# Two transformer blocks on one core: the values of the second block's layers computed with tokens in rows, in 512-column products

## The reference

```python
h = rms_norm_2(x, pre_norm[l]) @ w_in[l]          # 256 x 3072, split in ten parts
dq, dk, dv, dgate, gq, gk, gv, ggate, mq, mgate = ...
# D: 6 heads of differential attention (two softmaxes a head, q and k of 32), rope on dq and dk
oa = rms_norm_2(diff_attention(q1, q2, k1, k2, dv, lam), diff_subln[l]) * silu(dgate)
# G: 6 query heads of 64 on 2 key/value heads, rms norm and axial rope on gq and gk
ob = gqa_attention(gq, gk, gv) * silu(ggate)
# M: 4 heads that read a memory of 256 rows
om = softmax(mq @ mk.T / 8) @ mv * silu(mgate)
x = x + rms_norm_2(concat(oa, ob, om) @ w_out[l], post_norm[l])
```

## Time and profile before

| | before |
|---|---|
| median of three runs | 712.62 us (711.74 to 713.48) |
| span of the profiled execution | 709.0 us |
| PE busy | 640.6 us (90%) |
| DVE busy | 354.9 us (50%) |
| ACT busy | 331.0 us (47%) |
| POOL busy | 45.9 us (6%) |

### The profile page before, as it was taken

How to read it: one execution, slowest core, us unless ns; L and a number is a source line. 1 busy time by engine, 2 the same in 40 slices (tenths; PEclk the granted TensorE clock), 3 DMA queues, 4 the chain that set the end, 5 groups by cost and what they waited for, 6 DMA issues and landing times.

```text
span 709.0 us, 11877 instructions
## 1 busy us (share of the span) xinstructions
PE 640.6 (90%) x4645; PEld 491.1 (69%) x4646; DVE 354.9 (50%) x820; ACT 331.0 (47%) x782; POOL 45.9 (6%) x57
## 2 busy tenths in 40 slices
PE   5989999999999999778686899999989999999996
PEld 4967898779743345323242589878878898888886
DVE  1543657555740131011010448889775577897743
ACT  3465655641120132111120344779865546888842
POOL 6001000000000000000000233010000020100000
PEclk9999999999999999897899999999999999999999
DMA  9994335597999999999999938018533071093101
GB/s 288 328 320 150 119 119 178 172 330 275 367 361 414 389 419 409 415 410 415 410 413 413 323 121 279 18 42 256 179 119 119 2 238 60 1 297 119 61 1 59
DMA packets 82169, 166.80 MB, mean 235 GB/s; under 512 B 4286, under 2 KB 59360, under 8 KB 78016
## 3 DMA queue, kind: packets, MB, share of 16 engines
q1 hardware_dynamic: 79984, 160.88, 62.8%
q0 software_dynamic: 2000, 5.06, 2.2%
q10 hardware_dynamic: 128, 0.08, 0.0%
HBM read 164.92 MB, written 1.07 MB: 234 GB/s over the span
## 4 chain that ended last, share of the span: by engine, by line
PE 59%; SPq 16%; DVE 9%; DMA 6%; ACT 6%; issue 3%; DVEq 0%; ACTq 0%
SPq L805 13%; PE psum L941 11%; PE psum L943 10%; PE psum L942 10%; PE psum L996 4%; DMA ring<-in_w_in_dram 3%; DMA ring<-in_w_expert_down_dram 3%; PE psum L1367 3%; PE psum L1258 3%; SPq L808 3%; PE psum L1305 2%; PE psum L1323 2%; DVE w_low L2414 2%; PE psum L1382 2%; PE psum L1350 2%
## 5 line engine op out<-in xcount | busy, mean ns | idle before, releaser
L941 PE MATMUL psum<-a_high,w_high 128*128 128x256 f32 x512 | 149.5, 292 | 5.4 <-ACT tiles L1617 1.7
L942 PE MATMUL psum<-x_low,w_high 128*128 128x256 f32 x512 | 144.7, 283 | 0.0
L943 PE MATMUL psum<-a_high,w_low 128*128 128x256 f32 x512 | 144.6, 283 | 0.0
L2414 DVE TENSOR_TENSOR w_low<-ring,w_high 128x1024 fp32r<-128x1024 f32 (+1 forms) x73 | 100.9, 1395 | 28.3 <-ACT w_high L1728 28.3
L941 PEld LDWEIGHTS psum<-a_high,w_high 128*128 128x128 f32 x512 | 97.8, 191 | 15.7 <-issue 7.2
L1728 ACT ACTIVATE w_high<-ring 128x1024 fp32r<-128x1024 f32 (+1 forms) x79 | 96.2, 1222 | 13.9 <-DMA ring<-in_w_in_dram 10.5
L942 PEld LDWEIGHTS psum<-x_low,w_high 128*128 128x128 f32 x512 | 98.0, 191 | 0.1
L943 PEld LDWEIGHTS psum<-a_high,w_low 128*128 128x128 f32 x512 | 98.0, 191 | 0.0
L1367 PE MATMUL psum<-ring,q_c 128*32 128x512 f32 x304 | 63.8, 700 | 22.3 <-DMA ring<-in_w_expert_up_dram 10.6
L941 PE MATMUL psum<-w_high,a_high 128*128 128x256 f32 x240 | 69.9, 291 | 1.8 <-DVE mix_low L2425 1.4
L2336 DVE TENSOR_TENSOR tiles<-tiles,psum 128x256 f32<-128x256 f32 x8 | 3.4, 421 | 127.5 <-ACT tiles L1784 127.5
(11 more groups left out here) (347 smaller groups left out, 1204.9 us busy)
## 6 DMA issues: line engine op xcount, KB each, us to landing
ring<-in_w_in_dram SPq DMA_DIRECT2D x36, 1024.0 KB, 8.0
ring<-in_w_expert_down_dram SPq DMA_DIRECT2D x24, 1024.0 KB, 17.0
ring<-in_w_expert_gate_dram SPq DMA_DIRECT2D x38, 512.0 KB, 14.7
ring<-in_w_expert_up_dram SPq DMA_DIRECT2D x38, 512.0 KB, 15.0
ring<-in_w_out_dram SPq DMA_DIRECT2D x12, 1024.0 KB, 5.4
ring<-in_w_mem_kv_dram SPq DMA_DIRECT2D x4, 1024.0 KB, 14.7
probs_values<-in_w_expert_down_dram SPq DMA_DIRECT2D x3, 1024.0 KB, 18.9
k_c<-in_w_expert_gate_dram SPq DMA_DIRECT2D x5, 512.0 KB, 8.9
```

The costliest lines, as they stand in the source:

```text
L941: pe.matmul(dst, left[0], right[0], start=first, stop=False)
L942: pe.matmul(dst, left[0], right[1], start=False, stop=False)
L943: return pe.matmul(dst, left[1], right[0], start=False, stop=last)
L2414: dve.tensor_tensor(w_l, raw_of(n), as_f32(w_h), ALU.subtract).then_inc(lows, 1)
```

## The change

The values are no longer four turned tiles with transposes. Two jobs `("nv", l, tt)`, one for each half of the tokens, compute all 512 value columns for 128 tokens: the tokens' high and low parts are the stationary operand, and the moving operand is one chunk of all four tiles' weights, 512 columns in four blocks of 128, which lie in four neighbouring places. It is again `product`, so 24 matmuls a job. ACT evicts the whole bank in one instruction. The weights of a value tile are split as before, now as `("v2", l, n)`, and all four splits must be there for the first job. The `nv` jobs stand in the turns of D0 and D1, tile 15 moves to D2, and its `hsq` and rope move back by a turn. `exchange` moves from D4 to D5. Column block 8 of the weights (with tile 16) is loaded before block 7.

```diff
-LOAD_ORDER2 = [0, 1, 2, 3, 4, 7, 8, 6, 9, 10, 5, 11]
+LOAD_ORDER2 = [0, 1, 2, 3, 4, 8, 7, 6, 9, 10, 5, 11]
...
-        tiles = [[6, 7], [8, 15], [16, 12], [13], [14], [17, 9], [18], [20], [19], [10], [22], [21], [11], [23], [], []]
+        tiles = [[], [], [15, 12], [13], [14], [17, 9], [18], [20], [19], [10], [22], [21], [11], [23], [], []]
+        values = [[("nv", l, 0)], [("nv", l, 1)]] + [[]] * (len(tiles) - 2)
...
-                if t in V_TILES:
-                    behind[n + 1].append(("vn", l, t))
...
-            turns.append((before[n] + [("tile2", l, t) for t in tiles[n]] + behind[n], s))
+            turns.append((before[n] + values[n] + [("tile2", l, t) for t in tiles[n]] + behind[n], s))
...
-LONG = ("tile1", "bv", "tile2", "mv")
+LONG = ("tile1", "bv", "tile2", "nv", "mv")
...
-        _at = max(_at, users(_n - 3)[0])
+        _at = max(_at, users(_n - (5 if SPLITS[_n][0] == "v2" else 3))[0])
...
+        def values_split(l, k):
+
+            a = units_before(SPLIT[("v2", l, V_TILES[0])]) % UNITS
+            assert a + len(V_TILES) <= UNITS
+            return [w[:, KC * P * a:KC * P * (a + len(V_TILES))].rearrange("p (n k q) -> p n k q", n=len(V_TILES), k=KC)
+                    [:, :, k, :] for w in (w_high, w_low)]
...
+            def values_product(dst, l, tt):
+
+                pe.wait_ge(lows, SPLIT[("v2", l, V_TILES[-1])] + 1)
+                own = slice(P * tt, P * tt + P)
+                for k in range(KC):
+                    mm = product(dst, (a_high3[:, k, own], x_low3[:, k, own]), values_split(l, k), k == 0, k == KC - 1)
                 return mm
...
-                elif kind == "vn":
-                    l, n = job[1:]
-                    from_act(("tile2", l, n))
-                    for tt in range(2):
-                        mm = pe.transpose(dst[:, P * tt:P * tt + P], tile3[:, n, P * tt:P * tt + P], ident)
+                elif kind == "nv":
+                    mm = values_product(dst, job[1], job[2])
...
-                elif kind == "vn":
-                    l, n = job[1:]
-                    op = act.activation(v2[:, :, V_TILES.index(n), :], src[:, 0:256].rearrange("p (t n) -> p t n", t=2),
-                                        ACT.Copy)
+                elif kind == "nv":
+                    op = act.activation(v_nat[:, 512 * job[2]:512 * job[2] + 512], src, ACT.Copy)
...
-                dve.wait_ge(p_act, taken(JOB[("vn", l, 16)]))
...
-                    if what[0] == "D" and what[2] == 4:
+                    if what[0] == "D" and what[2] == 5:
                         exchange(what[1])
```

More of the change, by code:

```diff
@@ L351, in item_of @@
         return [f"mem_{kind[1]}{job[1]}"]
-    if kind == "tile2":
+    if kind in ("tile2", "v2"):
         return [f"in{job[1]}_{job[2] // 2}"]
@@ L368 @@
 A_Q_TILES = (("tile1", 0), ("tile1", 1))
-OF_TILES, OF_ITEMS = ("tile1", "tile2"), ("bv", "y1", "y2")
+OF_TILES, OF_ITEMS, ONE_UNIT = ("tile1", "tile2"), ("bv", "y1", "y2"), ("tile1", "tile2", "v2")
 SPLITS = []
 for _job in JOBS:
-    _what = _job if _job[0] in OF_TILES else _job[:-1] if _job[0] in OF_ITEMS else None
-    if _what and _what not in SPLITS:
-        SPLITS.append(_what)
+    if _job[0] == "nv":
+        _parts = [("v2", _job[1], t) for t in V_TILES]
+    else:
+        _parts = [_job] if _job[0] in OF_TILES else [_job[:-1]] if _job[0] in OF_ITEMS else []
+    SPLITS += [what for what in _parts if what not in SPLITS]
 SPLIT = {what: n for n, what in enumerate(SPLITS)}
-UNIT_OWNER = [n for n, what in enumerate(SPLITS) for _ in range(1 if what[0] in OF_TILES else 2)]
+UNIT_OWNER = [n for n, what in enumerate(SPLITS) for _ in range(1 if what[0] in ONE_UNIT else 2)]
 def units_before(split):
@@ L385, in users @@
     what = SPLITS[split]
+    if what[0] == "v2":
+        return [JOB[("nv", what[1], tt)] for tt in range(2)]
     return [JOB[what]] if what[0] in OF_TILES else [JOB[what + (tt,)] for tt in range(2)]
@@ L395, in item_split @@
 def item_split(split):
-    return ITEM[item_of(SPLITS[split] if SPLITS[split][0] in OF_TILES else SPLITS[split] + (0,))[0]]
+    return ITEM[item_of(SPLITS[split] if SPLITS[split][0] in ONE_UNIT else SPLITS[split] + (0,))[0]]
 LAST_INPUT = max(n for n, _job in enumerate(JOBS) if _job[0] in ("tile1", "bv"))
@@ L508, in split_of @@
         def split_of(n):
-            wide = P if SPLITS[n][0] in OF_TILES else COLS
+            wide = P if SPLITS[n][0] in ONE_UNIT else COLS
             a = units_before(n) % UNITS * KC * P
@@ L522, in raw_of @@
                 return s.rearrange("p k (g m d) -> p k m g d", g=2, m=2)[:, :, what[1]]
-            return s[:, :, P * (what[-1] % 2):P * (what[-1] % 2) + P] if what[0] in OF_TILES else s
+            return s[:, :, P * (what[-1] % 2):P * (what[-1] % 2) + P] if what[0] in ONE_UNIT else s
         def split_like_raw(n):
@@ L966, in natural_product @@
                 return mm
+            def values_product(dst, l, tt):
[3 more added lines that the diff above has]
+                    mm = product(dst, (a_high3[:, k, own], x_low3[:, k, own]), values_split(l, k), k == 0, k == KC - 1)
+                return mm
             def output_product(dst, job, phase):
@@ L1274, in run_out @@
                 elif kind == "D":
-                    from_act(("vn", l, 6 + h // 2))
+                    from_act(("nv", l, 1))
                 elif kind == "G":
-                    from_act(("vn", l, 16))
+                    from_act(("nv", l, 1))
                 else:
```

## The result

| | before | after |
|---|---|---|
| median of five runs, us | 711.87 (711.13 to 713.48) | 715.93 (714.01 to 716.33) |
| span of the profiled execution, us | 709.0 | 714.3 |
| first product of tile 0, layer 0 and layer 1, us | 420.50, 566.59 | 422.32, 570.50 |
| from there to the first product of tile 20, us | 67.50, 66.81 | 69.66, 68.27 |

The ratio is 1.0058, with a 95% interval of 1.0039 to 1.0077: slower, by 4.1 us. The forecast was 710.8, and the time lies above its range.

What follows compares the result with a forecast made beforehand. In the heads D the chain was PE to D4's scores, DVE to D5's maxima, then ACT. Gains of 1.1 and 0.4 us, 0.5 more if DVE's normalization shortens, were put at 1.8: 710.8, range 707.5 to 713.7.

Steps and rivals of the forecast that it cites:

- D4's scores: PE's scores of head D4, expected 2 to 3 us earlier relative to the layer's opening; 2.55 in layer 0.
- Opening: Before D0's scores: two more low parts on DVE, 2.28 us, delay the scores 0.57 us in layer 0, 0.8 in layer 1.
- The two jobs: PE's values products at 222 ns, 10.66 us the pair; D2's scores start 2.7 us earlier.
- The wait before tile 13: PE waits a new 1.7 us for tile 13's low part, which DVE reaches only after D3's maxima.
- Rival B: Nothing comes out: DVE bounds from the opening, or the wait before tile 13 is 2.5 us; 712.6, chance 0.25.
- DVE from the maxima of D4 to those of D5: Exchange moves out, tile 15's rope comes in: 8.7 us instead of 7.25, giving back 1.45 of the gain.
- Tile 20: Its start at the end of the heads D: 1.1 us earlier in layer 0, 0.4 in layer 1.
- Rival A: DVE keeps up in the heads D, so PE's full saving stays: about 4.1 us a layer, 704.5; chance 0.08.
- Rivals C and D: Values products: C, four-block operand read slowly, 444 ns, 732, chance 0.06; D, width costs nothing, 120 ns, about 701, chance 0.03.
- Rival E: Tile 16's low part comes late; first values job waits a further 1.5 us in each layer: 714.5, chance 0.08.

Runs made afterwards that it cites:

- the best variant: Changed kernel with tile 13's split queued at the second values' job, and tile 15's sum of squares and rope one turn earlier: 705.69 us, ratio 0.9921.
- the second edit: Tile 15's sum of squares moved to D2's turn and its rope to D3's; alone in the changed kernel: 716.18 us, ratio 1.0066 to the kernel before.
- the narrow variant: Changed kernel with each product of 512 columns made as two of 256: 716.47 us, ratio 1.0073 to the kernel before.

## Why the prediction was wrong

A gain was forecast and a loss came, so it isn't only a matter of size. The chain was the one forecast, and the new wait is where it was put, but three terms of DVE's and PE's part were too small, and a fourth, the clock behind the new wait, was put at nothing without a reason. All four go in the same direction and use up the gain at D4's scores, which was one of the prediction's own signs. In the order of its steps:

1. **Opening**: +0.57 and +0.8 us for D0's scores were forecast, +1.02 (18.97 after the first product against 17.95) and +1.39 came; the first job came +1.16 and +1.55 later, not +0.6 and +0.9. The step counted low parts at 1.14 us. Three of them stand in a row beside a product of POOL and take 4.03 where 3.42 were counted, and the ropes behind them move as well. Taking POOL's product away gives 0.6 and 0.9 back, and D0's scores then come 0.42 us later than before the change in layer 0, where 0.57 were forecast.
2. **The two jobs**: 228 ns a product and 11.0 us the pair, not 222 and 10.66. The scores of D2 came 1.85 us earlier, not 2.7. Of the 0.85, 0.56 are the opening's and 0.3 the spacing's.
3. **The wait before tile 13**: 2.45 us, not 1.7. Tile 13 had its low part 9.99 us after D2's scores began, not 9.15, and of the 0.84 the stretched rows at 459.70 and 462.18 are 0.37 and 0.41. With POOL's product cut it is 9.21 us and the wait 1.68, which is the forecast. Rival B named a wait of 2.5 us, but priced it at no gain, since it left the other terms as they were.
4. **D4's scores**: 2.55 us earlier were forecast in layer 0, and they came 0.66 later (48.71 against 48.05 us after the first product). Steps 1 to 3 are 1.7 of the difference. The other 1.5 is the **half clock behind the new wait**, which the prediction didn't have at all. In layer 1, where the clock held, 1.8 us earlier were forecast, and they came at the same time within 0.1 (47.32 against 47.37).
5. **DVE from the maxima of D4 to those of D5**: forecast 8.7 us, measured 8.74. The 1.45 given back was right. With nothing gained at D4's scores there was nothing to give it back from, and it is layer 1's whole loss of 1.46 us.

Tile 20 was forecast at 1.1 and 0.4 us earlier and came 2.16 and 1.46 later. The sum of +3.6 is the measured +4.1 within the scatter. Rival A's premise, that DVE keeps up if its order allows, is what the best variant comes near to, with 6.1 us of the 8 that A names, by an order that also has the second edit. Rivals C and D fall by the spacing of 228 ns. Rival E, slower by a little, is nearest in the number, but its wait isn't there: the first job follows D0's scores by 1.22 us, against 1.08 before. The Trainium skill, "TensorE: Matmul & The Clock Gate", section "Back-to-back issue gap", has 216 ns for this width by its formula for an isolated product, and the trace lies 12 ns above it, and 11 ns above it for 256 columns (120 against 109).

What failed is the treatment of DVE's chain. Once a chain by one engine sets the end, each small stretching of its rows counts in full. The prediction took the rows at the length that they had in the kernel before, where POOL's products (432.85, 453.30, 462.04) weren't beside them, and didn't ask where the new order would put those products. And it counted what PE loses by waiting 1.7 us, but not what the clock may take from the products behind the wait.

## What to carry to other kernels

Before saving work on the bound engine, write down for each operand that it needs next when the other engine can deliver it; here one split queued one job too late made the difference between a gain of 2 us and a loss of 4. A wait on PE also has a price behind it, when the clock falls; and where a chain of small operations becomes the path, cost it with what another engine does beside it. An edit that moves work to an earlier turn has to be checked against what stands behind it in that turn: the same one gave 4.2 us with the low part out of the way, nothing without that, and took 3.3 in the kernel before.

## What was not expected of the hardware

**The clock after a wait.** After 2.45 us of waiting the granted clock fell in layer 0 of the changed kernel and not in its layer 1, nor in either layer of the narrow variant. After 3.90 us it fell in both layers, and after 1.68 in neither. Late in layer 0 all thirteen profiled kernels, the two of the change included, have the same wait of 1.63 us (1.64 in one). In seven of them the clock fell behind it, and tile 20 to layer 1 takes 78.5 to 78.6 us; in the other six it stayed at full, and the same stretch takes 77.5. The runs don't show what decides, and 1.1 us of the difference between two profiled executions can be no more than this.

**DVE beside POOL.** Beside a 128x256 product of POOL (0.72 to 0.88 us), two operations of DVE on 128x256 took 1.25 us instead of 0.88, a 128x4 one 0.58 instead of 0.17, and three low parts 4.03 instead of 3.52. POOL's own product takes up to 1.6 us beside a low part, as at 438.84 us of the changed kernel. Cut to 16 columns it takes 0.22 us at 431.54 and 1.07 at 438.01, beside a low part that began at 437.79 and took 1.22: it ends with that low part, and DVE's 0.58 us end with POOL's product at 462.7. That looks as if one instruction waited for the other to end, more than as if both ran slower; POOL's spans are rough, and no run tests it. The Trainium skill, "GPSIMD Engine Reference", section "Specifications", says that GpSimd shares its SBUF interfaces with VectorE and that they contend with operations of two SBUF inputs or of a two-port mode. The cut of POOL's product, after which DVE's rows were short again, agrees with it; no run here tells the two kinds apart.
